# Mixer heads: the denominator's division folded into the group norm's root, floors and denominators in token quarters

## The reference, cut to what matters

```python
def mlstm_chunkwise(q, k, v, ig, lf):
    ...
        m_t = jnp.maximum(g, jnp.max(logw, axis=-1))
        w = jnp.exp(logw - m_t[..., None])
        ...
        s = jnp.einsum("bhtd,bhsd->bhts", qc, kc) * w
        num = jnp.einsum("bhts,bhse->bhte", s, vc) + inter[..., None] * ...
        den = jnp.sum(s, axis=-1) + inter * ...
        h = num / jnp.maximum(jnp.abs(den), jnp.exp(-m_t))[..., None]

def group_layer_norm(x, n_groups, g, b=None):
    ...
    mu = jnp.mean(xf, axis=-1, keepdims=True)
    xc = xf - mu
    var = jnp.mean(xc * xc, axis=-1, keepdims=True)
    y = (xc * lax.rsqrt(var + EPS)).reshape(shp) * g.astype(jnp.float32)

def mixer(...):
    ...
    h_m = mlstm_chunkwise(q, k * (Dh ** -0.5), v, ig, lf)
    h_m = group_layer_norm(h_m.reshape(B, T, D_MLSTM), H, g_mh)
    h_m = jax.nn.sigmoid(z) * h_m
    a = glu_a * jax.nn.sigmoid(glu_b)
    a = causal_depthwise_conv(a, w_dw, b_dw)
    a = jax.nn.silu(group_layer_norm(a, N_CONV_GROUPS, g_cn, b_cn))
    return jnp.concatenate([h_m, a], axis=-1) @ w_out
```

## Time and profile before

| | us |
|---|---|
| median of 3 runs | 2341.88 (2338.35 to 2342.68) |
| the profiled execution's own time | 2337.8 |
| its span, first to last instruction | 2335.9 |
| PE busy | 2273.5 (97%) |
| DVE busy | 1321.0 (57%) |
| POOL busy | 1103.3 (47%) |
| ACT busy | 967.0 (41%) |
| mean granted clock of PE | 0.987 |

### The profile page before, as it was taken

The page is one execution under the profiler, slowest core; times in us unless marked ns, Lnnn a source line. Parts: engine busy times, 40 slices in busy tenths (PEclk is TensorE's granted clock), DMA queues, the critical chain, the costliest instruction groups (busy, mean ns, idle before and its releaser), DMA issues.

```text
span 2335.9 us, 29041 instructions
## 1 busy us (share of the span) xinstructions
PE 2273.5 (97%) x10642; PEld 1809.5 (77%) x10642; DVE 1321.0 (57%) x2073; ACT 967.0 (41%) x1546; POOL 1103.3 (47%) x561
## 2 busy tenths in 40 slices
PE   7999899999999999999999999999999999999998
PEld 5886667788888888766787888887768788888886
DVE  4999866862442789995566022057676754221222
ACT  3368443332232334875344133144654453332332
POOL 2697423634434638883364444463422234444442
PEclk9999999899999999999999999999999999999999
DMA  8532203544555523221122233232211122332322
GB/s 310 171 98 67 63 19 132 178 142 155 163 169 164 168 68 97 83 82 37 46 83 80 90 100 98 90 106 72 82 55 55 55 72 91 100 99 90 104 94 90
DMA packets 206660, 240.38 MB, mean 103 GB/s; under 512 B 9762, under 2 KB 172378, under 8 KB 206554
## 3 DMA queue, kind: packets, MB, share of 16 engines
q1 hardware_dynamic: 206554, 238.97, 32.4%
HBM read 236.84 MB, written 2.10 MB: 102 GB/s over the span
## 4 chain that ended last, share of the span: by engine, by line
PE 53%; DVE 4%; ACT 2%; issue 1%; DMA 0%; POOL 0%; DVEq 0%; ACTq 0%; SPq 0%
PE product L2473 16%; PE product L2475 15%; PE product L2474 15%; DVE side L1835 1%; PE product L3055 1%; PE side L3023 1%; PE side L3043 1%; PE product L2830 1%; PE side L2542 0%; PE side L2806 0%; DVE slot_f L1835 0%; PE side L2970 0%; PE side L2566 0%; ACT sqt L1407 0%; DMA ring_f<-in_w_out 0%
## 5 line engine op out<-in xcount | busy, mean ns | idle before, releaser
L940 POOL TENSOR_TENSOR ring_low<-ring_f,ring_high 128x1024 fp32r<-128x1024 f32 (+1 forms) x349 | 847.3, 2433 | 1078.2 <-ACT ring_high L1050 1077.8
L2473 PE MATMUL product<-slot_r,ring_high 128*128 128x512 f32 (+1 forms) x2536 | 1009.4, 398 | 18.0 <-ACT slot_f L1248 3.4
L2475 PE MATMUL product<-slot_r,ring_high 128*128 128x512 f32 (+1 forms) x2536 | 990.5, 391 | 0.0
L2474 PE MATMUL product<-slot_r,ring_low 128*128 128x512 f32 (+1 forms) x2536 | 989.7, 390 | 0.0
L1050 ACT ACTIVATE ring_high<-ring_f 128x1024 fp32r<-128x1024 f32 (+1 forms) x349 | 368.0, 1057 | 684.9 <-DMA ring_f<-in_w_ff 336.3
L2473 PEld LDWEIGHTS product<-slot_r,ring_high 128*128 128x128 f32 (+1 forms) x2536 | 476.8, 188 | 151.0 <-issue 37.0
L2475 PEld LDWEIGHTS product<-slot_r,ring_high 128*128 128x128 f32 (+1 forms) x2536 | 476.8, 188 | 102.1
L2474 PEld LDWEIGHTS product<-slot_r,ring_low 128*128 128x128 f32 (+1 forms) x2536 | 477.5, 188 | 96.9 <-issue 1.4
L1794 DVE SCALAR_TENSOR_TENSOR va<-product,sqt 128x512 f32<-128x512 f32 x96 | 66.3, 692 | 350.7 <-ACT sqt L1122 349.4
L1835 DVE SCALAR_TENSOR_TENSOR side<-slot_f,cols,side 128x512 f32<-128x512 f32 x326 | 217.2, 747 | 0.0
L1812 DVE TENSOR_TENSOR slot_f<-product,slot_f 128x512 f32<-128x512 f32 x64 | 44.2, 690 | 182.1 <-PE product L2475 182.1
(11 more groups left out here) (322 smaller groups left out, 2245.0 us busy)
## 6 DMA issues: line engine op xcount, KB each, us to landing
ring_f<-in_w_ff SPq DMA_DIRECT2D x128, 512.0 KB, 3.9
slot_f<-in_w_ada SPq DMA_DIRECT2D x48, 1024.0 KB, 6.9
ring_f<-in_w_in SPq DMA_DIRECT2D x96, 512.0 KB, 3.9
ring_f<-in_w_out SPq DMA_DIRECT2D x40, 512.0 KB, 3.5
ring_f<-in_w_up SPq DMA_DIRECT2D x32, 512.0 KB, 3.7
ring_f<-in_w_down SPq DMA_DIRECT2D x32, 512.0 KB, 3.7
slot_f<-in_x SPq DMA_DIRECT2D x4, 512.0 KB, 5.1
ring_f<-in_w_v SPq DMA_DIRECT2D x4, 512.0 KB, 3.8
```

What stands on the lines that cost most here:

```text
L940: pool.tensor_tensor(whole(ring_low[:, s, :, :], n), whole(ring_f[:, s, :, :], n), whole(ring_high[:, s, :, :], n).bitcast(F32), ALU.subtr ...
L2473: pe.matmul(out_ap, high, rhs_high, start=start, stop=False)
L2474: pe.matmul(out_ap, low, rhs_high, start=False, stop=False)
L2475: return pe.matmul(out_ap, high, rhs_low, start=False, stop=stop)
```

## The change

The value tiles are no longer divided by d. What goes with it and what comes instead:

- `floor_columns`, `floor_wide`, `floored` and `scaled` are gone, for each of the 4 heads of a layer. `m_row` is gone with its four small transposes; the stabilizer's sums are written by four instructions into `floor_rows`, a tile of 128 x 128 in which row 32 s + h holds head h's tokens of quarter s.
- The denominator is summed by four `quarter_sums` into the first 128 columns of `PM[1]`, quarter s of the array for token quarter s, row hd for head hd; it is added up over the heads.
- `floor_squares`, once for all heads, makes eps d^2 from it on 128 x 128; one more DVE instruction adds it to the variance of the undivided values; ACT's root has no scale and bias any more, and `inverse_root` runs on its own.
- `head_gate` and `head_squares` read the value banks themselves, and `head_gate` is what frees them. It stands after `weighted(h + 1, 0)` and `(h + 1, 1)`, for head 0 also after `conv_low(6, 7)`. `head_squares(0)` moves into ACT's silu loop.
- `head_vars` puts token quarter s in quarter s and head hd in row hd, where it was the reverse; the root's spread is issued in four turns of four, each in four banks and four quarters, and each turn waits for the one before.

```diff
                 def denominator(hd):
 
-                    wait(pe, place, floor_ready, hd + 1)
-                    pe.matmul(PM[1][:, 0:P], ones[:], prob[:, 0, 0:P], start=True, stop=True)
+                    wait(pe, place, p_ready, 4 * hd + BLK)
                     wait(pe, place, prob_added, 3 * hd + 3)
-                    pe.matmul(PM[1][:, P:T], ones[:], prob_sum(hd)[:, P:T], start=True, stop=True).then_inc(head_done.sem, 1)
+                    for s in range(BLK):
+                        sums = prob[:, 0, 0:P] if s == 0 else prob_sum(hd)[:, s * P:(s + 1) * P]
+                        ins = quarter_sums(PM[1], s, hd, sums, hd == 0, hd == HEADS - 1)
+                    ins.then_inc(head_done.sem, 1)
...
-                wait(pe, place, den_ready, HEADS)
-                for s in range(BLK):
-                    for hd in range(HEADS):
-                        ins = quarter_spread(PM[hd][:, s * P:(s + 1) * P], hd, s)
-                        if s == BLK - 1:
-                            ins.then_inc(hrn_ready.sem, 1)
+                for turn in range(HEADS):
+                    if turn:
+                        wait(pe, place, hrn_ready, BLK * turn)
+                    for s in range(BLK):
+                        hd = (s + turn) % HEADS
+                        quarter_spread(PM[hd][:, s * P:(s + 1) * P], s, hd).then_inc(hrn_ready.sem, 1)
...
                 def head_squares(h):
                     for e in range(2):
                         t = 2 * h + e
-                        wait_taken(act, place, o_head(h, e))
-                        act.activation(head_square(t), tile(SG, t), ACT.Square).then_inc(sqn_ready.sem, 1)
+                        wait(act, place, head_done, 3 * h + e + 1)
+                        act.activation(head_square(t), bank(o_head(h, e))[:], ACT.Square).then_inc(sqn_ready.sem, 1)
...
-                wait(act, place, hm_var, HEADS)
-                deviation(place, PM[3][:, 0:P], 2 * P, hroot_ready)
+                wait(act, place, hvar_ready, 1)
+                act.activation(root[:], PM[3][:, 2 * P:3 * P], ACT.Sqrt).then_inc(hroot_ready.sem, 1)
...
                 def head_gate(h):
                     for t in (2 * h, 2 * h + 1):
+                        o = o_head(h, t % 2)
                         wait(dve, place, sqn_ready, t + 1)
-                        dve.scalar_tensor_tensor(tile(SG, t), tile(SG, t), cols[:, V_GMH + t:V_GMH + t + 1],
-                                                 tile(SE, t), ALU.mult, ALU.mult).then_inc(hz_ready.sem, 1)
+                        dve.scalar_tensor_tensor(tile(SG, t), bank(o)[:], cols[:, V_GMH + t:V_GMH + t + 1],
+                                                 tile(SE, t), ALU.mult, ALU.mult).then_inc(taken[o % 4].sem, 1)
+
+                def floor_squares():
...
+                    met, found = floor_rows[:], PM[1][:, 0:P]
+                    steps.did(dve.scalar_tensor_tensor(met, found, -1.0, met, ALU.mult, ALU.max))
+                    steps.wait()
+                    steps.did(dve.tensor_tensor(met, found, met, ALU.max))
+                    steps.wait()
+                    steps.did(dve.tensor_scalar(met, met, MOST, EPS ** 0.5, ALU.min, ALU.mult))
+                    steps.wait()
+                    steps.did(dve.tensor_tensor(met, met, met, ALU.mult))
...
                 conv_low(2)
-                floored(0)
                 conv_normed(5)
                 conv_low(3)
                 conv_normed(6, 7)
                 conv_low(4, 5)
-                scaled(0)
                 weighted(1, 0)
                 weighted(1, 1)
                 conv_low(6, 7)
+                head_gate(0)
                 for h in range(1, HEADS):
                     weighted(h, 2)
                     weighted(h, 3)
                     if h < HEADS - 1:
                         diagonal(h + 1)
-                    floored(h)
                     if h < HEADS - 1:
                         weighted(h + 1, 0)
                         weighted(h + 1, 1)
-                    scaled(h)
-                    head_gate(h - 1)
-                head_gate(3)
+                    head_gate(h)
+                met = floor_squares()
+                wait(dve, place, hm_var, HEADS)
+                v, q = (PM[3][:, k * P:(k + 1) * P] for k in (2, 3))
+                dve.scalar_tensor_tensor(v, PM[3][:, 0:P], 1.0 / (2 * P), met, ALU.mult, ALU.add).then_inc(hvar_ready.sem, 1)
                 wait(dve, place, hroot_ready, 1)
...
-                refine(PM[3], 2 * P, P, hrn_small)
+                inverse_root(v, q, root[:], inv_cols[:], hrn_small)
```

More of the change, by code:

```diff
@@ L41 @@
 EPS = 1e-6
+MOST = 1e18
 DVE_GROUP = 21
@@ L369, in program @@
         row_pick = sb("row_pick", [P, 8])
+        floor_rows = sb("floor_rows", [P, P])
         sqt = sb("sqt", [P, 2, T])
@@ L1009, in _ @@
                     low_part(place, LAYER, i)
-                wait(pool, place, hz_ready, NT)
+                for e in range(2):
+                    wait_taken(pool, place, o_head(HEADS - 1, e))
                 pool.memset(region_f[:, SE:SE + SLOT], 0.0).then_inc(y_cleared.sem, 1)
@@ L1321, in decay @@
                     act.activation(wexp[j][:, 0:P], dg[j], ACT.Exp).then_inc(w_ready.sem, 1)
-                def floor_wide(h):
-                    wait(act, place, tap_used, TAPS)
-                    wait(act, place, floor_spread, h + 1)
-                    act.activation(tap[h], PM[1][:], ACT.Copy).then_inc(floor_ready.sem, 1)
                 def conv_share(t):
@@ L2135, in _ @@
                 wait(dve, place, crn_ready, NT)
-                refine(PM[3], 2 * P, P, hrn_small)
-                wait(dve, place, hz_ready, NT)
-                wait(dve, place, hrn_ready, HEADS)
+                inverse_root(v, q, root[:], inv_cols[:], hrn_small)
+                for e in range(2):
+                    wait_taken(dve, place, o_head(HEADS - 1, e))
+                wait(dve, place, hrn_ready, BLK * HEADS)
                 def head_low(t):
@@ L2766, in _ @@
                 gate_product(2)
-                wait(pe, place, mrow_ready, 1)
+                wait(pe, place, mrow_ready, BLK)
                 settled(pe)
                 for s in range(BLK):
-                    for n, row in enumerate((a_row, m_row)):
-                        at = (n * BLK + s) * HEADS
-                        ins = pe.transpose(PM[1][:, at:at + HEADS], row[:, s * P:(s + 1) * P], ident[0:HEADS, 0:HEADS])
+                    ins = pe.transpose(PM[1][:, s * HEADS:(s + 1) * HEADS], a_row[:, s * P:(s + 1) * P],
+                                       ident[0:HEADS, 0:HEADS])
                 ins.then_inc(acol_done.sem, 1)
@@ L2898, in head_vars @@
                     wait(pe, place, pair_sums, heads[-1] + 1)
[L2899 to L2903 removed]
+                    for hd in heads:
+                        for s in range(BLK):
+                            ins = quarter_sums(PM[3], s, hd, head_square(2 * hd)[:, s * P:(s + 1) * P], hd == 0, hd == HEADS - 1)
+                        ins.then_inc(hm_var.sem, 1)
                 head_vars(0, 1, 2)
```

75 lines of the change are left out of this document (24 added, 51 removed).

## The result

The changed kernel takes 2350.07 us (median of 10 runs, 2347.55 to 2358.41), the kernel before 2340.95 us (10 runs, 2335.36 to 2344.39): 9.1 us slower, ratio 1.0037 with a 95% interval of 1.0025 to 1.0048. I had forecast 2339.0 us, within 2334.0 to 2344.4, most likely no change that can be measured. The profiled execution after took 2351.75 us, with a span of 2350.0 and a mean granted clock of 0.981, where it was 0.987.

The account below looks back on a forecast made before the run. PE was taken to bound the kernel, full in heads 1 to 3 but waiting in head 0. Layer 0's -2.05 and layer 1's -0.85 gave -2.9 us, from 2341.88 to 2339.0, range 2334.0 to 2344.4.

Parts of the forecast that it names:

- Heads 1 to 3: Where PE is full, dropping the floor's spread and shortening the denominator sums was to save 3.9 us per layer.
- `conv_product(0)` 1.9 sooner: In head 0, less PE work and fewer DVE passes were to start this product 1.9 us earlier (ends 1.0, 2.3).
- The bank released late: Head 1's first values wait 3.8 us for head_gate(0) instead of 1.02: net +0.9 us in layer 1, +0.5 in layer 0.
- the collision: Ahead of head 1, DVE's two conv lows meet POOL's sum of squares: +0.4 us per layer (ends 0, +1.4).
- The clock after the wait: Behind head 1's wait PE runs at 1.2 GHz for a stretch: +1.65 us per layer, chosen from 0, 1.65, 3.35.
- The tail: At variance and root, an earlier root (-0.46 us) against a spread in four turns (+0.85): together +0.4 us in layer 1.
- Layer 0's credit of -0.7: In layer 0 a later PE wait for a ring low was to end 0.7 us sooner and hide the spread's turns.
- The small transposes: Four instead of eight: -0.3 us in layer 1, nothing in layer 0; the four sums priced about like the one replaced.
- the slower one: Rival, chance 0.10: at the wait for head_gate(0) the clock falls and stays low through most of head 1; 2347 us or more.
- No clock loss, no collision: Rival, chance 0.30: PE keeps full clock through head 1's wait, DVE and POOL do not clash; -7.0 us, 2334.9.
- The quarters did overlap: Denies the rival of denominator quarters running one after another: +0.9 us, 2342.8; chance 0.15 shared with gains given back.

Follow-up runs that it names:

- the gate first: The changed kernel with head_gate(0) moved ahead of weighted(1, 0), where DVE waits for ACT's weights: 2336.78 us, ratio 0.9981 to the kernel before.

## Why the prediction was wrong, point by point

The forecast was -2.9 us and the measured change +9.1, 12 us apart. The worth of the removed work in heads 1 to 3, where PE is full, was right, and so was the place of the new wait. What failed is what the waits cost: the clock behind the late release was put at 1.65 per layer and took 2.7, head 0's clock was put at nothing and took some 2.1 on average, from a cause that stays open, the wait itself was longer than counted, and the credits for layer 0 and for the transposes have the wrong sign.

*Heads 1 to 3, -3.9 per layer*: right. At full clock B to V went from 47.4 to 43.65, -3.75, and the quarter sums took the 0.43 worked out for them.

*`conv_product(0)` 1.9 sooner*: 1.33 where the clock is full. The step that failed is one that I didn't take: I let head 0 run at the clock it had. With the stretches counted above, 2.5 against 0.4 us per layer, A to P is 0.8 longer on average instead of 1.9 shorter. That average is over seven executions of five kernels; in the changed kernel's own four layers A to P is 20.0 against 19.9 in eight of before.

*The bank released late, a wait of 3.8*: 4.74 in both layers. The place and the gate's 1.41 were right (1.40). The lows took 2.20 instead of 1.28, where I had put 0.4 for the collision and 1.4 at the far end. From P to B it is 3.4 more than before.

*The clock after the wait, +1.65 per layer, "the middle one"*: 2.4 to 2.9 in both profiles of the changed kernel, 2.7 on average, and gone when PE was kept busy through the same wait. This term and the missing one in head 0 make 4.8 per layer (2.7 + 2.1) instead of 1.65, half of the 12 us between forecast and result.

*The tail, +0.4*: V to S fell by 0.45, as worked out (0.46); the turns cost 1.34 instead of 0.85.

*Layer 0's credit of -0.7*: wrong in sign. I took the wait for `ring_low` at 415.42 for the one that decides. PE's timelines at the norm's start behind the output product, of the kernel before and then of the changed one:

```profile
438.92 1.95 PE L2566 MATMUL side<-ones,slot_f 128*128 128x1 f32 x16 [0.72 <-POOL slot_f L953]
```

```profile
444.49 3.57 PE L2561 MATMUL side<-ones,slot_f 128*128 128x1 f32 x16 [4.56 <-POOL slot_f L949]
```

Counted from E (379.04 and 384.40) the norm starts at 59.9 and 60.1: DVE's and POOL's chain from the spread on sets it, and what PE gains in between it waits for. In all 20 profiled executions, of whichever kernel, it lies between 59.0 and 60.4, while E itself lies anywhere from 376.3 to 389.9. So what moves E by more than that spread counts. For the turns' 1.33 it is not shown: the 60.4 belongs to the execution without them. And from E to the first product of the MLP the changed kernel takes 83.7 and 83.3, before 81.0 to 82.2: 1.9 more, with the lower clock in the norm for 17.1 us instead of 10.2 to 13.7. What the longer wait has to do with that was not tried by itself.

*The small transposes, -0.3 in layer 1*: wrong in sign, and in both layers. They are 0.27 shorter, as worked out, but wait 0.65 for DVE's four sums, which I had put at the price of the one they replace: 3.13 instead of 1.61. From the start of the product ahead of them to that of the product behind, PE takes 1.34 and 1.36 instead of 0.90, some +0.45 per layer, and nothing up to head 0 takes that back: from the product behind to A it is 49.57 in layer 0 and 42.51 in layer 1, in the profile of either kernel.

*The sum by rows*, per layer: +0.45 (transposes) - 1.3 + 2.1 (head 0 and its clock) + 3.4 (P to B) - 1.05 (B to V, low clock included) - 0.45 + 1.35 = +4.5; twice that and 1.9 for layer 0's norm is 10.9, where 9.1 was measured (5.9 to 11.2 by the interval of the ratio). With A to E of the changed kernel's own four layers, 92.8 against 89.5 in eight of before, it is 9.3. Ahead of the first large product executions of either kernel differ by up to 5 us (its start lies at 30.5 to 33.8 in the five with the floor, at 30.4 to 35.2 in the fifteen without it); whether the change has a part in that stays open, and the sum leaves it out.

*The rivals*: the slower one named the mechanism, the clock at the wait for `head_gate(0)`, but asked 10.9 us at the lower clock behind it; it was 6.8, 4.8 to 5.9 of them with work. That its time, 2347 or more, came true is in part luck: head 0's stretch, the longer wait and the norm, none of which it named, made up the rest. "No clock loss, no collision" came in neither profiled execution of the changed kernel; nearest to it is the gate first, without the wait, -4.8 instead of -7.0. The quarters did overlap (0.43, not 1.06).

## What to carry to other kernels

When a change alters which instruction frees a buffer, look at what stands ahead of it in its engine's list, not only at how long it takes: here a 1.4 us gate stood behind an instruction that waited 4.25 us, and moving it ahead of that wait turned 0.37% slower into 0.19% faster. An idle time of PE is to be priced with the clock behind it (here 4.7 us and 2.7 more). Work taken from PE in a stage where it also waits need not be worth its own length: head 0 gained 1.33 us where the clock was full, and lost more than that where a low stretch came, whose cause stays open. One instruction split into four can make PE wait for the last of them (3.13 us instead of 1.61). A wait that is seen on PE may only be the first of several for one chain: compare the distance from the chain's start to a later mark before giving credit for it.

## What the runs showed of the hardware that I had not expected

A TENSOR_SCALAR of 128x128 in the floor's squares took 2.27 us. DVE's timeline of the changed kernel, layer 0:

```profile
375.47 0.29 DVE L2069 TENSOR_TENSOR floor_rows<-side,floor_rows 128x128 f32<-128x128 f32 x1
375.80 2.27 DVE L2071 TENSOR_SCALAR floor_rows<-floor_rows 128x128 f32<-128x128 f32 x1
378.10 0.29 DVE L2073 TENSOR_TENSOR floor_rows<-floor_rows 128x128 f32<-128x128 f32 x1
...
379.96 0.95 DVE L1637 RECIPROCAL inv_cols<-root 128x128 f32<-128x128 f32 x1 [1.23 <-ACT root L1365]
```

POOL made a ring low from 375.60 for 2.39 us, to 377.99, and the TENSOR_SCALAR ended at 378.07; the one on a PSUM bank took 0.30. It ate most of the cover that I had counted for the floor's passes; the root was still not held up by them, since the last pass ended at 378.73 and DVE waited 1.23 us more for ACT, which was at a ring copy. The Trainium skill, SBUF — State Buffer, section "Who interferes with whom", says that a tensor_scalar can use both port pairs and is then shut out by a GpSimd instruction that came first; the row agrees. By the same section's rule on two SBUF inputs the lows were to lose up to 1.0 beyond my 0.4 in each layer; they lost 0.92 in all.

The low stretches come and go between executions of one kernel: the changed kernel's two profiled executions had that of head 0 in different layers. Which of them comes is not explained here.
